# A different order of projection tiles in the second half of each group's round: B, C, x, x, z, z

## The chip, the core and the metric

The kernel runs on one core of one Trainium2 chip. The metric is the device time of one execution in microseconds (us); lower is better. TensorE (PE in the rows) does the matrix products, VectorE (DVE), ScalarE (ACT) and GpSimd (POOL) work on 128-partition tiles, and SyncE (SP) issues most transfers. Each engine works through its own list of instructions in order, and engines wait for each other by semaphores.

## What is computed

One layer of a diffusion trunk for 128 context and 1024 latent tokens, 1152 in all, of width 1024. What matters here is the mixer with its two branches, and how its inputs are made from one projection:

```python
proj = h @ lw["w_in"]
xbc, z, dt_raw, hq, hf, hi, hg, gate_logits = jnp.split(proj, cuts, axis=-1)
xbc = silu(depthwise_conv5(xbc) + conv_b)      # along a row of 64 tokens (latent)
xs, bm, cm = jnp.split(xbc, [...])             # x, B, C of the SSD branch
y = ssd_scan(xs, dt, a, bm, cm, s0)            # forward and backward, 8 groups
y = y * jax.nn.silu(z)
y = group_rmsnorm(y, ssd_norm_w)
o = hgrn2_scan(silu(hq), log_f, k, hi, s0)     # forward and backward, 8 heads
```

x, B and C go through a five-tap convolution and silu; z goes through silu alone. The convolution and the closing silu of x, B and C are elementwise work for ScalarE and VectorE, some five times that of z.

## The kernel before

**Stages.** `setup` makes the normalised input `h` in a high and a low float part. `mixers` is the stage of this change. After it `merge_and_ffn` and `last_norm` do the output projections, the feed-forward part and the last norm; the change does not touch them.

**Rounds and slots.** `mixers` goes over 8 groups, seven in a hardware loop (`Fori`) and the last one written out behind it. A round has a first half, stage A, and a second half, stage B, of 18 slots each. In every slot TensorE first computes one *unit* of projection (`project`: a 128-column weight tile times 384 tokens, as 24 matmuls, eight slices of the contraction times three combinations of high and low parts) and then a slice of recurrent work. Three units make one *tile* of the projection, one weight tile over all 1152 tokens.

**What runs beside what.** In stage A the recurrent work is the SSD scan of this group (`ssd`), and the projections make the inputs of this group's HGRN branch. In stage B the recurrent work is the HGRN scan (`hgrn`), and the projections make z, B, C and x of the next group. The last group's stage B has no next group and projects gate columns, with a tanh in the place of the convolution. The HGRN work is 33 steps (`STEPS`), two in a slot (`slot_of`), so that it falls into three blocks of five slots: block 0 in slots 1 to 5, block 1 in slots 6 to 10, block 2 in slots 11 to 15; slots 16 and 17 hold little. For each step GpSimd makes the argument (L1665 to L1686), ScalarE its Exp (L1110), VectorE a product (L1474), TensorE a small matmul (L818), and VectorE merges the result (L1462, L1465). `hs_b` and `hs_f` are the chunk states; their updates (L1443) follow matmul L848. TensorE may run only two of the merged results ahead (`lv_used`, L815).

**How a unit of stage B is evacuated.** Two PSUM banks take the units in turn (`bank_free`). For a z unit ScalarE takes a tanh from the bank (L955) and VectorE multiplies it with the bank (L1310), which frees it. For a convolution unit ScalarE copies the bank to `pad` (L939), which frees it, and makes the first tap (L946); VectorE adds four taps (L1303); ScalarE takes the tanh of the result one slot later (`conv_tanh`, L921), before the Exps of that slot; VectorE closes with a product (`conv_silu`, L1290), before its HGRN work of that slot.

**The order around it.** All orders are written out by hand: `CONV_TILES` says which of the six tiles are convolved, `B_COLS` and `PRO_COLS` which columns are loaded in turn, `b_dest` where a tile goes. Weights come by SyncE into two buffers (`raw`), are cast to the high part by ScalarE (L914) and split by VectorE (L1277, once per tile in its second slot); TensorE waits for the split at the tile's first unit. At the start of stage B ScalarE makes `rstd` and VectorE norms y into `x_t` (`ssd_norm`, L1376), after which SyncE stores `x_t` (`stores`). At the end of stage B ScalarE makes the rstd of the HGRN branch (L1115, L1118), VectorE norms o (L1484, L1486), ScalarE stores it (L1123); only then do the loop's back edge and stage A of the next round come on ScalarE. Ahead of the loop a *prologue* makes dt and the same six tiles for group 0, without recurrent work beside them.

Of the kernel before, what the change touches and what calls it, by code (L numbers as in the profile page):

```python
# [12 lines left out]
P = 128  # L13
# [5 lines left out]
NB = 3  # L19
# [85 lines left out]
            eng.wait_ge(self.sem, self.g * self.per + (self.before + self.n))  # L105


CONV_TILES = (2, 3, 4, 5)


def conv_index(k):

    return k - 2 * NB


def b_tile(k):
# [77 lines left out]
def setup(nc, scope, sb, sem, m):  # L194
# [40 lines left out]
    with nc.Block() as block:  # L235
        @block.sync
        def _(sp):
            sp.dma_start(cst[:, :], m["cst_in"]).then_inc(consts_in, 16)
            sp.dma_start(junk[:, 0:LEVELS * P], m["masks_in"].rearrange("p l i -> p (l i)")).then_inc(masks_in, 16)

            def row(part, col, src, n):
                sp.dma_start(rows[part:part + n, col, :], src).then_inc(rows_in, 16)

            row(0, 0, m["ssd_conv_w"][0, 0:4, :].rearrange("k (t p) -> (k t) p", p=P), 128)
            row(0, 1, m["ssd_conv_w"][0, 4, :].rearrange("(t p) -> t p", p=P), 32)
            row(32, 1, m["ssd_conv_b"][0].rearrange("(t p) -> t p", p=P), 32)
            row(64, 1, m["ada_b"][0].rearrange("(t p) -> t p", p=P), 48)
            row(112, 1, m["norm_mix_w"][0].rearrange("(t p) -> t p", p=P), 8)
            row(120, 1, m["norm_ffn_w"][0].rearrange("(t p) -> t p", p=P), 8)
            row(0, 2, m["ssd_norm_w"][0].rearrange("(t p) -> t p", p=P), 16)  # L250
            row(16, 2, m["hgrn_norm_w"][0].rearrange("(t p) -> t p", p=P), 8)
            row(24, 2, m["c_in"][0].rearrange("(t p) -> t p", p=P), 8)
            row(32, 2, m["c_ctx"].rearrange("(t p) -> t p", p=P), 8)

            sp.dma_start(d_all[:, :], m["ssd_d"][0].rearrange("(a h) -> a h", a=1).broadcast_to([P, 32])
                         ).then_inc(rows_in, 16)
            def load_ada(j):
                sp.dma_start(ada[j % 3][:, :, :], ada_w[:, j * ADA_T * P:(j + 1) * ADA_T * P]
                             .rearrange("(k p) c -> p k c", p=P)).then_inc(ada_in[j % 3], 16)

            for c in range(3):
                sp.dma_start(xt[c][:, :], x_rows(c)).then_inc(x_in[c], 16)
                load_ada(c)

            for i, (col, n) in enumerate(((COL_DT, HD), (COL_Z, P))):
                sp.dma_start(raw[i][:, :, 0:n], m["w_src"](m["w_in"][0], col, n)).then_inc(m["w_landed"][i], 16)
            for j in range(3, ADA_N):
                sp.wait_ge(ada_used, j - 2)
                load_ada(j)
                if j < NC:  # L270
                    sp.wait_ge(x_turned, j - 2)
                    sp.dma_start(xt[j % 3][:, :], x_rows(j)).then_inc(x_in[j % 3], 16)
# [177 lines left out]
def mixers(nc, scope, sb, sem, m):  # L450
# [133 lines left out]
        n = TILES_BEFORE + t  # L584
        return n % 2, g * (TILES_GROUP // 2) + n // 2, g * TILES_GROUP + n

    PRO_COLS = [(COL_DT, 64), (COL_Z, P), (COL_Z + P, P), (COL_B, P), (COL_C, P), (COL_X, P), (COL_X + P, P)]

    A_COLS = [(COL_FF, P), (COL_FB, P), (COL_Q, P), (COL_G, P), (COL_GATE, P), (COL_I, P)]
    B_COLS = [(COL_Z, GW), (COL_Z + P, GW), (COL_B, P), (COL_C, P), (COL_X, GW), (COL_X + P, GW)]  # L590


    with nc.Block() as block:
        @block.sync
        def _(sp):
            def load(g, t, col, width=P):
                i, _, n = tile(g, t)
                if not (g is None and t < 2):
                    sp.wait_ge(w_split.sem, n - 1)
                sp.dma_start(raw[i][:, :, 0:width], w_src(w_in, col, width)).then_inc(w_landed[i], 16)  # L600

            def stage_a(g):
                for t, (base, step) in enumerate(A_COLS):
                    load(g, t, g * step + base)

            def stores(g, last):

                sp.wait_ge(y_final, g + 1)
                dst = y_dram[2 * g:2 * g + 2] if isinstance(g, int) else y_dram[bass.ds(g * 2, 2)]
                sp.dma_start(dst.rearrange("t p n -> p t n"), x_t[:, :, :]).then_inc(y_stored, 16)  # L610

                hs = slice(HPG * g, HPG * (g + 1)) if isinstance(g, int) else bass.ds(g * HPG, HPG)
                for d in range(2):
                    sp.dma_start(m["new_ssm"][0, 0, d, hs].rearrange("(t e) p n -> (e p) t n", e=2),
                                 st_in[:, 2 * d:2 * d + 2, :]).then_inc(so_stored, 16)

            def store_h(g):
                sp.wait_ge(kc_used.sem, kc_used.at(g, 4))
                hh = slice(g, g + 1) if isinstance(g, int) else bass.ds(g, 1)
                for d in range(2):  # L620
                    sp.dma_start(m["new_hgrn"][0, 0, d, hh].rearrange("a k v -> k (a v)"),
                                 so_h[:, d, :]).then_inc(soh_stored, 16)

            sp.dma_start(cols[:, 0:1], m["ssd_dt_bias"][0].rearrange("d (h a) -> (d h) a", a=1)
                         ).then_inc(cols_in, 16)
            sp.dma_start(cols[:, 1:2], m["ssd_a_log"][0].rearrange("d (h a) -> (d h) a", a=1)
                         ).then_inc(cols_in, 16)
            sp.dma_start(acc[0][:, 0:2 * P], m["neg_in"].rearrange("p d i -> p (d i)")).then_inc(cols_in, 16)
            for t, (col, _) in enumerate(PRO_COLS):
                if t >= 2:  # L630
                    load(None, t, col)

            with sp.Fori(0, G - 1) as g:
                stage_a(g)
                for t, (base, step) in enumerate(B_COLS):
                    if t == 4:
                        stores(g, False)
                    load(g, 6 + t, g * step + (base + step))
                store_h(g)
            g = G - 1  # L640
            stage_a(g)
            for t in range(8):
                if t == 4:
                    stores(g, True)
                load(g, 6 + t, COL_GATE + D + t * P)
            store_h(g)

            last_tile = tile(G - 1, 13)[2]
            for i in range(2):
                sp.wait_ge(w_split.sem, last_tile + i)  # L650
                slot = (last_tile + 1 + i) % 2
                sp.dma_start(raw[slot][:, :, :], w_src(m["w_ssd_out"][0, 0:D, :], slot * P)
                             ).then_inc(m["m_w_in"][slot], 16)
            sp.wait_ge(y_stored, 16 * G)

            sp.wait_ge(so_stored, 32 * G)
            sp.wait_ge(soh_stored, 32 * (G + 1))
            sp.wait_ge(o_stored, 16 * (G + 1))
            for i in range(2):
                sp.wait_ge(gate_stored[i], 16 * (G * (1 + i) + 4 * NB))  # L660
# [241 lines left out]
        def _(act):  # L902
# [20 lines left out]
            def b_evac(g, k):  # L923
# [24 lines left out]
                                   ).then_inc(tap_done.sem, 1)  # L948
                else:

                    if k >= 2:
                        act.wait_ge(bank_free[ui], used)
                    elif g is not None:
                        act.wait_ge(v_turned, g * NB + (k + 2))
                    act.activation(th[ui][:, :], bank[:, 0:BW], ACT.Tanh, scale=0.5).then_inc(th_ok.sem, 1)  # L955

            def b_th_free(g, k):

                ci = conv_index(k)
                if ci >= 2:  # L960
                    wait(silu_done, g, ci - 1)

            def a_evac(g, k):
                t, b = divmod(k, NB)
# [224 lines left out]
            for k in range(SLOTS):  # L1189
# [3 lines left out]
                b_evac(None, k)  # L1193
                if k % NB == 0:
                    high(None, k // NB + 2) if k < SLOTS - NB else high(0, 0)
            b_th_free(None, SLOTS - 1)
            conv_tanh(None, SLOTS - 1)
            act.wait_ge(dt_turned, 1)
            flat = tok[:, :, :, :].rearrange("p a c r -> p (a c r)")
            for i in range(4):  # L1200
# [7 lines left out]
            def stage_b(g):  # L1208
                for k in range(SLOTS):
# [10 lines left out]
                        hgrn_rstd(g)  # L1220
                    if k % NB == 0:
                        high(g, 6 + k // NB + 1)
                b_th_free(g, SLOTS - 1)
                conv_tanh(g, SLOTS - 1)
                store_o(g)

            with act.Fori(0, G - 1) as g:
# [32 lines left out]
        def _(dve):  # L1260
# [18 lines left out]

            def b_dest(k):  # L1280
                t, b = b_tile(k)
                return (z_t[:, 0, blk(b)], z_t[:, 1, blk(b)], b_t[:, blk(b)], c_t[:, blk(b)],
                        x_t[:, 0, blk(b)], x_t[:, 1, blk(b)])[t]

            def conv_silu(g, k):
                ui = b_unit(g, k)[0]
                wait(th_ok, g, k + (0 if g is None else 2 * NB) + 1)
                if k == 12 and g is not None:
                    dve.wait_ge(y_stored, g * 16 + 16)
                dve.scalar_tensor_tensor(b_dest(k), th[ui][:, :], 1.0, acc[ui][:, :], ALU.add,  # L1290
                                         ALU.mult).then_inc(silu_done.sem, 1)
# [254 lines left out]
            for k in range(SLOTS):  # L1546
# [2 lines left out]
                b_evac(None, k)  # L1549
                if k % NB == 1:  # L1550
                    low(None, k // NB + 2) if k < SLOTS - NB else low(0, 0)
            conv_silu(None, SLOTS - 1)
            ch = dve_s

            with dve.Fori(0, G - 1) as g:
                ch.round(g)
                stage_a(g)
                for k in range(SLOTS):
# [7 lines left out]
                        hgrn_norm(g)  # L1566
                    if k % NB == 1:
                        low(g, 6 + k // NB + 1)
                conv_silu(g, SLOTS - 1)
                assert ch.n == DVE_ROUND, ch.n  # L1570
            g = G - 1
            ch.round(g)
# [627 lines left out]
```

## Time and profile before

| | us |
|---|---|
| median of 3 runs | 3678.38 (3676.9 to 3679.32) |
| span of the profiled execution | 3671.7 |
| TensorE busy | 3388.0 (92%) |
| VectorE busy | 1775.6 (48%) |
| ScalarE busy | 1386.3 (38%) |
| GpSimd busy | 810.5 (22%) |
| mean granted clock of TensorE | 0.971 |

The profiled execution took its span of 3671.7 us; the median is 6.7 us above that, which lies around the span. The busy shares are means over stages with different limits: the mixer stage lies between about 145 and 2352 us of the span, and seven of its eight rounds have convolutions in stage B. In a timeline row the first two numbers are the start and the time that the instruction or a merged run of them took; what stands in brackets is the idle time of the engine before it and what ended it. In a row of stretches the numbers are the length, then the busy time of each engine.

### The profile page before, as it was taken

To read this page: it belongs to the slowest core of one execution; us is meant where nothing else is said; L and a number is where in the kernel's file an instruction comes from. 1 tells how busy PE (TensorE), PEld (TensorE's weight loads), DVE (VectorE), ACT (ScalarE), POOL (GpSimd) and SP (SyncE) were. 2 spreads that over 40 slices of the span, in tenths; PEclk is the share of its full clock that TensorE was granted. 3 is DMA by queue.
4 is the path that set the end of the run, shared out by engine and by line. 5 is a ranking of instruction groups with operands and counts; after the bars stand their busy time and mean duration, and the time that the engine had idled before them with its cause. 6 is when DMAs were issued, how large, how long until landed. Compare 5 with 4: busy or idle time off the path is not lost. (4 is left out here: it accounts for less than half of the span.)

```text
span 3671.7 us, 56487 instructions
## 1 busy us (share of the span) xinstructions
PE 3388.0 (92%) x19856; PEld 3225.1 (88%) x19856; DVE 1775.6 (48%) x2918; ACT 1386.3 (38%) x2655; POOL 810.5 (22%) x1138
## 2 busy tenths in 40 slices
PE   7789989989989889899899899899998999999997
PEld 2379979889889889889889899799997999999997
DVE  2455566556656746745755764334434222222233
ACT  4334444454554454454544545321124110120112
POOL 0002532532622613524425325000010000000000
PEclk9999999999999999999999999999998999999998
DMA  8310111111111111111111112344231111111111
GB/s 312 102 35 24 47 41 28 45 40 30 43 34 30 45 37 44 32 31 53 29 31 47 40 30 70 121 143 135 84 87 50 40 40 46 40 40 40 46 35 73
DMA packets 284854, 213.08 MB, mean 58 GB/s; under 512 B 10152, under 2 KB 266576, under 8 KB 284624
## 3 DMA queue, kind: packets, MB, share of 16 engines
q1 hardware_dynamic: 239808, 159.80, 14.5%
q10 hardware_dynamic: 44816, 50.35, 4.4%
q8 instruction: 128, 2.10, 0.2%
q14 instruction: 102, 0.84, 0.1%
HBM read 173.94 MB, written 36.18 MB: 57 GB/s over the span
## 5 line engine op out<-in xcount | busy, mean ns | idle before, releaser
L676 PE MATMUL bank<-h_hi,w_hi 128*128 128x384 f32 (+1 forms) x2520 | 892.5, 354 | 38.5 <-DVE z_t L1310 19.1
L676 PE MATMUL bank<-h_lo,w_hi 128*128 128x384 f32 (+1 forms) x2520 | 857.6, 340 | 0.0
L676 PE MATMUL bank<-h_hi,w_lo 128*128 128x384 f32 (+1 forms) x2520 | 856.6, 340 | 0.0
L676 PEld LDWEIGHTS bank<-h_hi,w_hi 128*128 128x128 f32 (+1 forms) x2520 | 484.6, 192 | 48.5 <-DVE z_t L1310 19.4
L1858 PE MATMUL bank<-a_hi,v_hi 128*128 128x384 f32 x1440 | 490.6, 341 | 33.8 <-DVE v_lo L1959 12.2
L676 PEld LDWEIGHTS bank<-h_lo,w_hi 128*128 128x128 f32 (+1 forms) x2520 | 483.3, 192 | 5.8
L1858 PE MATMUL bank<-a_lo,v_hi 128*128 128x384 f32 x1440 | 485.8, 337 | 0.0
L1858 PE MATMUL bank<-a_hi,v_lo 128*128 128x384 f32 x1440 | 485.7, 337 | 0.0
L676 PEld LDWEIGHTS bank<-h_hi,w_lo 128*128 128x128 f32 (+1 forms) x2520 | 481.9, 191 | 1.3
L1858 PEld LDWEIGHTS bank<-a_hi,v_hi 128*128 128x128 f32 x1440 | 273.3, 190 | 46.9 <-issue 35.6
L1858 PE MATMUL bank<-b_hi,v_hi 128*128 128x384 f32 x912 | 304.7, 334 | 0.5 <-DVE v_lo L1959 0.5
L1858 PE MATMUL bank<-b_hi,v_lo 128*128 128x384 f32 x912 | 304.6, 334 | 0.0
L1858 PE MATMUL bank<-b_lo,v_hi 128*128 128x384 f32 x912 | 304.6, 334 | 0.0
L1303 DVE SCALAR_TENSOR_TENSOR acc<-pad,taps,acc 128x384 f32<-128x384 f32 x384 | 274.2, 714 | 61.6 <-ACT acc L946 51.1
L1858 PEld LDWEIGHTS bank<-a_lo,v_hi 128*128 128x128 f32 x1440 | 274.2, 190 | 0.0
L1858 PEld LDWEIGHTS bank<-a_hi,v_lo 128*128 128x128 f32 x1440 | 273.9, 190 | 0.0
L1110 ACT ACTIVATE qk<-qk 128x768 f32<-128x768 f32 (+1 forms) x240 | 180.6, 777 | 187.8 <-POOL qk L1685 176.1
L1881 ACT ACTIVATE v_hi<-raw 128x1024 fp32r<-128x1024 f32 x99 | 104.8, 1059 | 295.4 <-PE bank L1858 289.2
L818 PE MATMUL bank<-qk 128*128 128x128 f32 x1008 | 142.0, 286 | 69.4 <-DVE at L1462 24.4
L818 PEld LDWEIGHTS bank<-qk 128*128 128x128 f32 x1008 | 132.7, 197 | 77.5 <-DVE at L1462 27.9
L1623 POOL TENSOR_TENSOR xp<-xb,tok_g 128x256 f32<-128x256 f32 x128 | 81.7, 646 | 500.2 <-PE bank L757 305.7
L2014 DVE TENSOR_TENSOR small<-small,bank 128x384 f32<-128x384 f32 x66 | 36.6, 554 | 295.4 <-PE bank L1858 295.4
(270 smaller groups left out, 5499.3 us busy)
## 6 DMA issues: line engine op xcount, KB each, us to landing
raw<-in_w_in SPq DMA_DIRECT2D x104, 512.0 KB, 3.9
raw<-in_ffn_w SPq DMA_DIRECT2D x60, 512.0 KB, 3.8
ada<-in_ada_w SPq DMA_DIRECT2D x12, 2048.0 KB, 9.3
small<-gate_scratch ACTq DMA_DIRECT2D x72, 192.0 KB, 2.4
gate_scratch<-th ACTq DMA_DIRECT2D x48, 192.0 KB, 1.9
y_scratch<-x_t SPq DMA_DIRECT2D x8, 1152.0 KB, 6.9
small<-y_scratch ACTq DMA_DIRECT2D x48, 192.0 KB, 2.4
raw<-in_w_ssd_out SPq DMA_DIRECT2D x16, 512.0 KB, 4.1
```

Source lines behind the costliest of these rows:

```text
L676: last = pe.matmul(out, w[i][:, k, 0:cols_n], h[:, k, blk(hb)], start=(k == 0 and j == 0), stop=(k == KT - 1 and j == 2))
L818: last = pe.matmul(S[(i + 1) % 3][:, chunk(j)], q[:, 1, chunk(j)], rhs, start=True, stop=True)
L1110: last = act.activation(v, v, ACT.Exp)
L1303: ins = dve.scalar_tensor_tensor(out, pad[b][:, :, j:j + GRID], taps[:, ti, j:j + 1], out, ALU.mult, ALU.add)
L1623: return pool.tensor_tensor(out.rearrange("p (h c) -> p h c", c=HD), x.rearrange("p (h c) -> p h c", c=HD), w.rearrange("p (h a) -> p h a" ...
L1858: last = pe.matmul(banks[3 * s + b][:, 0:BW], wp[s][:, k, :], operand[ap][:, k, blk(b)], start=(k == 0 and j == 0), stop=(k == kt - 1 and ...
L1881: act.activation(w_hi[s][:, :, :], raw[s][:, :, :], ACT.Copy).then_inc(w_high, 1)
L2014: dve.tensor_tensor(tmp[b][:, :], gate[b][:, :], bank, ALU.mult).then_inc(freed, 1)
```

## The change

In stage B and in the prologue the six tiles come as B, C, x, x, z, z, where they came as z, z, B, C, x, x. The four convolved tiles are then units 0 to 11 of the stage and z is units 12 to 17. What follows from it in the code:

- the column lists `PRO_COLS` and `B_COLS`, the first `COL_Z` load in `setup`, and `b_dest` are reordered;
- the store of y stands before the third load of a stage B on SyncE instead of before the fifth, since x is now written from unit 6 on;
- a convolution unit at the start of stage B (k of 0 and 1) waits in `b_th_free` for the turned v that z waited for; the first two z units wait in `b_evac` for the last two `conv_silu` instead;
- the last `conv_tanh` and `conv_silu`, which stood after the last slot, are gone: their unit now closes in slot 12.

No operation is added or left out, and the number of waits is about the same.

```diff
-CONV_TILES = (2, 3, 4, 5)
+CONV_TILES = (0, 1, 2, 3)
 def conv_index(k):
-    return k - 2 * NB
+    return k
...
-    PRO_COLS = [(COL_DT, 64), (COL_Z, P), (COL_Z + P, P), (COL_B, P), (COL_C, P), (COL_X, P), (COL_X + P, P)]
+    PRO_COLS = [(COL_DT, 64), (COL_B, P), (COL_C, P), (COL_X, P), (COL_X + P, P), (COL_Z, P), (COL_Z + P, P)]
-    B_COLS = [(COL_Z, GW), (COL_Z + P, GW), (COL_B, P), (COL_C, P), (COL_X, GW), (COL_X + P, GW)]
+    B_COLS = [(COL_B, P), (COL_C, P), (COL_X, GW), (COL_X + P, GW), (COL_Z, GW), (COL_Z + P, GW)]
...
-                    if t == 4:
+                    if t == 2:
                         stores(g, False)
...
-                    if k >= 2:
+                    if k >= 4 * NB + 2:
                         act.wait_ge(bank_free[ui], used)
-                    elif g is not None:
-                        act.wait_ge(v_turned, g * NB + (k + 2))
+                    else:
+                        wait(silu_done, g, k - 1)
...
                 if ci >= 2:
                     wait(silu_done, g, ci - 1)
+                elif g is not None:
+                    act.wait_ge(v_turned, g * NB + (k + 2))
...
-                b_th_free(g, SLOTS - 1)
-                conv_tanh(g, SLOTS - 1)
                 store_o(g)
```

On VectorE, the start of stage B in the loop, from the norm of y (`x_t`) to the split of the next weights (`w_lo`). Before, slots 0 and 1 hold one product `z_t` each between the HGRN products `qk`:

```order
L1376 SCALAR_TENSOR_TENSOR x_t<-x_t,vec_g,me 128x1152 x2
...
L1474 TENSOR_TENSOR qk1<-qk1,q_t 128x384
L1264 REGISTER_ALU
L1310 SCALAR_TENSOR_TENSOR z_t<-th1,bank1 128x384
L1264 REGISTER_ALU
L1474 TENSOR_TENSOR qk2<-qk2,q_t 128x384
...
L1310 SCALAR_TENSOR_TENSOR z_t<-th0,bank0 128x384
L1276 REGISTER_ALU
L1277 TENSOR_TENSOR w_lo0<-raw0,w_hi0 128x1024
```

And of the change, the same stretch (four taps `acc` in each slot, of which the last of each slot stands here, and the closing product of B):

```order
L1374 SCALAR_TENSOR_TENSOR x_t<-x_t,vec_g,me 128x1152 x2
...
L1301 SCALAR_TENSOR_TENSOR acc1<-pad2,taps,acc1 128x384
L1262 REGISTER_ALU
L1288 SCALAR_TENSOR_TENSOR b_t<-th1,acc1 128x384
L1262 REGISTER_ALU
L1472 TENSOR_TENSOR qk2<-qk2,q_t 128x384
...
L1301 SCALAR_TENSOR_TENSOR acc0<-pad1,taps,acc0 128x384
L1274 REGISTER_ALU
L1275 TENSOR_TENSOR w_lo0<-raw0,w_hi0 128x1024
L1262 REGISTER_ALU
L1288 SCALAR_TENSOR_TENSOR b_t<-th0,acc0 128x384
L1262 ISA
```

Eight taps and two closing products have taken the place of two products `z_t`, ahead of the first updates of `hs_b`. (The line numbers of the changed kernel are two or more lower here for VectorE and two higher for ScalarE.)

On ScalarE, the start of stage B in the loop; `ktok` are the turned keys that TensorE waits for. Before:

```order
L955 ACTIVATE th1<-bank1 128x384
L911 ISA
L913 ISA
L914 ACTIVATE w_hi0<-raw0 128x1024
L906 REGISTER_ALU
L1077 ACTIVATE ktok0<-bank4 128x384
```

And of the change:

```order
L939 ACTIVATE pad2<-bank1 128x6x64
L941 REGISTER_ALU
L942 REGISTER_ALU
L946 ACTIVATE acc1<-pad2,taps 128x384
L911 ISA
L913 ISA
L914 ACTIVATE w_hi0<-raw0 128x1024
L906 REGISTER_ALU
L1079 ACTIVATE ktok0<-bank4 128x384
```

A first tap has come ahead of the keys, and the tanh of that unit (L921, not shown) now follows the four keys and stands before the next Exps.

On ScalarE, the end of stage B in the loop, before, where the last tanh of a convolution stands between the rstd of the HGRN branch and the store of o:

```order
L946 ACTIVATE acc0<-pad0,taps 128x384
L906 REGISTER_ALU
L1115 ACT_TABLE_LOAD
L1115 ACTIVATE g_t<-g_t,cst 128x1152
L105 REGISTER_ALU
L1118 ACT_TABLE_LOAD
L1118 ACTIVATE g_t<-g_t 128x1152
L906 REGISTER_ALU
L921 ACTIVATE th0<-acc0 128x384
```

In the changed kernel the tanh of the last z unit stands straight before that rstd, and there is none behind it:

```order
L955 ACTIVATE th0<-bank0 128x384
L906 REGISTER_ALU
L1117 ACT_TABLE_LOAD
L1117 ACTIVATE g_t<-g_t,cst 128x1152
L105 REGISTER_ALU
L1120 ACT_TABLE_LOAD
L1120 ACTIVATE g_t<-g_t 128x1152
```

## Rows read from the trace of the kernel before

**Rows 1.** The page: head and busy times.

```profile
span 3671.7 us, 56487 instructions
PE 3388.0 (92%) x19856; PEld 3225.1 (88%) x19856; DVE 1775.6 (48%) x2918; ACT 1386.3 (38%) x2655; POOL 810.5 (22%) x1138
```

**Rows 2.** Groups by line: busy us, mean ns | idle before, releasers.

```profile
L676 PE MATMUL bank<-h_hi,w_hi 128*128 128x384 f32 (+1 forms) x2520 | 892.5, 354 | 38.5 <-DVE z_t L1310 19.1 <-DVE w_lo L1277 14.6 <-ACT dec L1205 4.8
...
L1303 DVE SCALAR_TENSOR_TENSOR acc<-pad,taps,acc 128x384 f32<-128x384 f32 x384 | 274.2, 714 | 61.6 <-ACT acc L946 51.1
...
L1310 DVE SCALAR_TENSOR_TENSOR z_t<-th,bank 128x384 f32<-128x384 f32 x48 | 26.3, 549 | 40.6 <-ACT th L955 40.6
```

**Rows 3.** Stretches, stage B of the second group: stretch length, PE, PEld, DVE, ACT, POOL, PEclk.

```profile
668.30:702.70 34.40, 31.32 (x212) 30.81 (x211) 22.32 (x39) 15.62 (x27) 25.81 (x36) 1.00 0.25 78
...
716.10:739.90 23.80, 19.67 (x120) 19.16 (x119) 21.04 (x31) 10.59 (x20) 10.96 (x14) 0.93 0.11 29
...
746.50:755.30 8.80, 6.01 (x39) 5.69 (x37) 6.37 (x11) 5.66 (x12) 8.56 (x13) 1.00 0.16 45
755.30:776.40 21.10, 19.36 (x116) 18.84 (x116) 19.02 (x31) 9.12 (x17) 2.71 (x2) 0.92 0.10 26
776.40:786.50 10.10, 9.24 (x54) 8.66 (x52) 5.21 (x8) 4.19 (x11) 0.00 (x0) 1.00 0.01 2
```

**Rows 4.** Stretches, the same slots of the last group's stage B, without convolutions.

```profile
2271.40:2288.90 17.50, 17.50 (x119) 17.50 (x119) 9.14 (x13) 7.05 (x11) 9.96 (x15) 1.00 0.25 76
...
2295.50:2301.30 5.80, 5.80 (x39) 5.66 (x37) 3.11 (x7) 2.80 (x5) 4.06 (x8) 1.00 0.10 34
2301.30:2318.50 17.20, 17.20 (x117) 17.20 (x116) 6.32 (x10) 5.71 (x9) 4.24 (x6) 1.00 0.27 82
2318.50:2327.50 9.00, 9.00 (x53) 8.73 (x52) 1.22 (x1) 5.25 (x8) 0.00 (x0) 1.00 0.28 88
```

**Rows 5.** Timeline of ACT, slot 0 of that stage B, keys and Exps of slot 1.

```profile
673.62 0.47 ACT L955 ACTIVATE th<-bank 128x384 f32<-128x384 f32 x1
...
674.93 1.62 ACT L1077 ACTIVATE ktok<-bank 128x384 f32<-128x384 f32 x4
...
676.63 1.60 ACT L1110 ACTIVATE qk<-qk 128x768 f32<-128x768 f32 x2
```

**Rows 6.** Timeline of DVE, slots 0 to 2: norm of y, states, first merge.

```profile
667.55 3.17 DVE L1376 SCALAR_TENSOR_TENSOR x_t<-x_t,vec_g,me 128x1152 f32<-128x1152 f32 x2 [16.25 <-ACT me L1066]
...
680.57 1.58 DVE L1443 SCALAR_TENSOR_TENSOR hs_b<-hs_b,hdec,bank 128x128 f32<-128x128 f32 x4
...
683.00 0.55 DVE L1462 TENSOR_TENSOR at<-bank,cst 128x384 f32<-128x384 f32 x1
```

**Rows 7.** Timeline of PE, the waits that end slots 1 and 2.

```profile
675.47 1.60 PE L818 MATMUL bank<-qk 128*128 128x128 f32 x12 [2.72 <-ACT ktok L1077]
...
683.61 0.60 PE L818 MATMUL bank<-qk 128*128 128x128 f32 x3 [0.36 <-DVE at L1462]
```

**Rows 8.** Timeline of DVE: four taps with POOL idle, four with POOL busy.

```profile
514.21 2.58 DVE L1303 SCALAR_TENSOR_TENSOR acc<-pad,taps,acc 128x384 f32<-128x384 f32 x4
...
717.66 3.96 DVE L1303 SCALAR_TENSOR_TENSOR acc<-pad,taps,acc 128x384 f32<-128x384 f32 x4
```

**Rows 9.** Timeline of ACT, the end of stage B into stage A, first round.

```profile
525.60 0.50 ACT L939 ACTIVATE pad<-bank 128x384 f32<-128x384 f32 x1
526.14 0.71 ACT L946 ACTIVATE acc<-pad,taps 128x384 f32<-128x384 f32 x1
...
539.20 0.38 ACT L1017 ACTIVATE s_f<-bank 128x256 f32<-128x256 f32 x1 [6.88 <-issue]
```

**Rows 10.** Timeline of PE, the wait in slot 1 of stage A, second round.

```profile
540.67 0.45 PE L683 MATMUL bank<-cst,x_t 128*128 128x128 f32 x2 [4.85 <-ACT xb L1025]
```

**Rows 11.** Stretch just behind that wait: length, PE busy, ..., PEclk.

```profile
541.60:548.50 6.90, 6.90 (x37) 6.79 (x35) 1.23 (x1) 4.45 (x10) 0.28 (x1) 0.80 0.30 77
```

**Rows 12.** The page: DMA issues, KB each, us to landing.

```profile
y_scratch<-x_t SPq DMA_DIRECT2D x8, 1152.0 KB, 6.9
```

More of the change, by code:

```diff
@@ L263, in _ @@
                 load_ada(c)
-            for i, (col, n) in enumerate(((COL_DT, HD), (COL_Z, P))):
+            for i, (col, n) in enumerate(((COL_DT, HD), (COL_B, P))):
                 sp.dma_start(raw[i][:, :, 0:n], m["w_src"](m["w_in"][0], col, n)).then_inc(m["w_landed"][i], 16)
@@ L1195, in _ @@
                     high(None, k // NB + 2) if k < SLOTS - NB else high(0, 0)
-            b_th_free(None, SLOTS - 1)
-            conv_tanh(None, SLOTS - 1)
             act.wait_ge(dt_turned, 1)
@@ L1281, in b_dest @@
                 t, b = b_tile(k)
-                return (z_t[:, 0, blk(b)], z_t[:, 1, blk(b)], b_t[:, blk(b)], c_t[:, blk(b)],
-                        x_t[:, 0, blk(b)], x_t[:, 1, blk(b)])[t]
+                return (b_t[:, blk(b)], c_t[:, blk(b)], x_t[:, 0, blk(b)], x_t[:, 1, blk(b)],
+                        z_t[:, 0, blk(b)], z_t[:, 1, blk(b)])[t]
             def conv_silu(g, k):
@@ L1287, in conv_silu @@
                 wait(th_ok, g, k + (0 if g is None else 2 * NB) + 1)
-                if k == 12 and g is not None:
+                if k == 2 * NB and g is not None:
                     dve.wait_ge(y_stored, g * 16 + 16)
@@ L1551, in _ @@
                     low(None, k // NB + 2) if k < SLOTS - NB else low(0, 0)
-            conv_silu(None, SLOTS - 1)
             ch = dve_s
@@ L1568, in _ @@
                         low(g, 6 + k // NB + 1)
-                conv_silu(g, SLOTS - 1)
                 assert ch.n == DVE_ROUND, ch.n
```

## The prediction

> **What bounds the kernel now.** I read the page first, then the groups of instructions by line, the waits of TensorE, and then the stages as stretches, slot by slot. TensorE is busy 3388.0 of 3671.7 us [rows 1], so a change of order can only act through the moments at which TensorE waits, or runs at a lower granted clock. For one of them the last round serves as a control, since its stage B runs the same HGRN slots without convolutions. Slots 8 to 10 take 23.8 us in the second group's stage B and 17.5 us in the last group's [rows 3, 4]: 6.3 us more, of which 1.7 us is a granted clock of 0.93 (0.07 of 23.8). Slot 12 takes 8.8 against 5.8 us (+3.0), slots 13 to 15 take 21.1 against 17.2 (+3.9), slots 16 and 17 take 10.1 against 9.0 (+1.1) [rows 3, 4]. In the control TensorE is busy without a gap in all of these. So a convolution beside an HGRN block costs TensorE time. VectorE shows why: it is busy 21.04 of the 23.8 us, against 9.14 of 17.5 [rows 3, 4]; it owes TensorE the HGRN products and merges, and pays them late. Six of these expensive slots with convolutions have z instead after the change, and six cheap ones get convolutions.
>
> **Part 1: block 0 gets the convolutions (slots 0 to 5).** Without them it takes 34.4 us, with VectorE busy 22.32 of it and GpSimd 25.81 [rows 3]. Two ways lead to its new length.
>
> By load: a convolution unit gives VectorE four taps of 714 ns, 2.86 us [rows 2]; its closing product has the shape of z's (549 ns) and replaces it. Five units are 14.3 us, and 22.32 + 14.3 = 36.6 us no longer fits 34.4: at least +2.2 us even with VectorE never idle. At the share of 0.88 at which it works in slots 8 to 10 (21.04 of 23.8), 36.6 us take 41.6, +7.2 us. Taps are also not 714 ns there: four take 2.58 us with GpSimd idle and 3.96 us beside it [rows 8], and in block 0 GpSimd works 75% of the time. With 3.96 us each the load is 22.3 + 19.8 = 42.1 us, at 0.88 47.8 us, +13.4 us.
>
> By chain: the start is more exposed than the other blocks. In slot 0 ScalarE now makes pad and first tap (0.5 and 0.71 us, [rows 9]) where one tanh of 0.47 us stood, so the keys at 674.93 [rows 5] come 0.7 us later; TensorE already waits 2.72 us for them [rows 7]: +0.7 us. In slot 1 ScalarE must wait for VectorE's first taps, which end at about 677.7 (first tap ready at 674.8, then 2.6 to 3.3 us), then makes the tanh (0.5), two Exps (1.60, [rows 5]), and the second unit's pad and tap (1.2), so that VectorE can start its second four taps at about 681.0. With 3.3 us for them (between 2.58 and 3.96), 1.2 for the split of the weights and 0.55 for the closing product, the chain of `hs_b` that started at 680.57 [rows 6] starts at about 686.1, 5.5 us later, and the first merge behind it, at 683.00, with it. TensorE waits only 0.36 us for that merge now [rows 7] and would wait some 5 us: the end of slot 2 moves by 5.4 us, the 0.7 included. Slots 3 to 5 hold the same step kinds as slots 8 to 10, so I take their +6.3. Together +11.7 us. This lies between the load's 7.2 and 13.4 and nearer to the latter, since GpSimd is busier here than in any other block. I take **+11.7**, bounds +4 (the load bound of 2.2, and some chain) and +16. What is queued behind the new waits: on ScalarE the load of the HGRN states and the Exps, for which VectorE's products and so TensorE wait; on VectorE the split of the next tile's weights, which moves from 680.6 to about 685.5 and is needed at the end of slot 2, so it is hidden by the longer slot 2.
>
> **Part 2: block 1 keeps them.** Its units are convolutions before and after: 0. VectorE enters it with a lag, but slots 5 and 6 hold few merges and absorb it. Slot 12 still sees the last convolution (unit 11), so its +3.0 stays.
>
> **Part 3: the end of stage B gets z.** Slots 13 to 17 lose 3.9 and 1.1 us [rows 3, 4]: **-5.0**. The control has no z product there; one of 549 ns a unit [rows 2] stays in for z, on a VectorE that has room (6.32 busy of 17.2, [rows 4]). Bounds -3.5 (part of it is clock, 0.92 of 21.1 us is 1.7) and -6.
>
> **Part 4: the turn into stage A.** ScalarE's last unit needs pad and tap before the rstd tables (1.2 us, [rows 9]) and then only a tanh of 0.47 to 0.49: 0.9 us earlier with everything behind it, the norm of o, its store, and the back edge; the copy at 539.20 had waited 6.88 us, named as issue [rows 9]. TensorE waits 4.85 us for the product of that chain [rows 10] and takes the gain in full: **-0.9**. The tanh and the closing product after the last slot were not in this chain. That stage A needs x_t, B and C at its first slots is no term: TensorE shows no wait there for `conv_silu`.
>
> **Part 5: SyncE's queue.** The load of the third tile, the first of x, now stands behind the store of y, which waits for `y_final`, at 667.55 + 3.17 = 670.7 [rows 6]. The store lands in 6.9 us [rows 12]; with as much again for the load, which is less than half as large, the weights are there at 684.5. The cast that needs them comes in slot 3, which began after the merge at 683.61 [rows 7] and will begin some 5 us later. Cost 0, covered by those 5 us; beyond them each us would be one of TensorE's.
>
> **Part 6: the prologue, once.** TensorE waits 19.1 us there for the first z product [rows 2]. That wait ends some 3 us earlier, as ScalarE's copy frees the bank instead; the first convolutions then start behind the dt chain and hold up the weight splits by about as much. At its end TensorE waits 4.8 us for `dec` [rows 2], behind the last tanh; with z last about 2 of them go. Net **-1**, bounds -5 and +5.
>
> **Part 7: the clock.** Behind the 4.85 us gap the granted clock is 0.80 over 6.9 us: 1.4 us lost [rows 10, 11]. The new gap in slot 2 is about as long, so I add 1.4 us x 7; the gap of part 4 shrinks to 3.95 us, for which I take back half of its loss: **+0.7** a round, bounds -2 and +3.
>
> **Sum.** A looped round: 11.7 - 5.0 - 0.9 + 0.7 = +6.5 us; seven of them +45.5, and -1 for the prologue: +44. The last round's stage B does not change. The profiled execution would take 3671.7 + 44 = 3716; with the 6.7 us that lie around the span, 3678.4 + 44 = **3722 us**, slower by 1.2%.
>
> **A rule weighed.** Four taps take 1.4 us longer beside GpSimd than alone [rows 8]. The Trainium skill, SBUF, "Who interferes with whom", says that a VectorE instruction with two SBUF inputs and a GpSimd instruction that reads SBUF exclude each other, and one with a single SBUF input does not. A tap reads pad and acc, both in SBUF; z's product reads one operand from PSUM. By that rule GpSimd's 25.8 us in block 0 and five times four taps at 2.58 us, 12.9 us, would have to be laid end to end: 38.7 us, +4.3 at least, on both engines. The rows agree in direction; the sum above does not use it.
>
> **Rivals.**
> *Hidden in idle VectorE (faster).* VectorE is idle for 12.1 of block 0's 34.4 us [rows 3], and GpSimd with 25.8 busy may be the pace-setter, so that convolutions fill holes. If block 0 grows by 2.8 us only (the load bound of 2.2 and little more), a round gains 3.1 us and the kernel takes 3656. It decides below +5.9 us for block 0, where parts 3 and 4 balance it. Against it: the holes are waits for ScalarE and GpSimd, the taps would stand ahead of what TensorE needs next, and in slots 8 to 10 the same mixture did not hide. Chance 0.12.
> *A draw.* Block 0 grows by 5 to 6.8 us, near the load figure of 7.2: the round changes by -0.9 to +0.9, 3671 to 3684. Chance 0.13.
> *A heavier start.* The port shared with GpSimd slows the arguments too, block 0 grows by 16, and the lag runs on into block 1: 7 x 4.3 more, 3752. Chance 0.15, of which 0.05 beyond 3756.
> *The late weights.* If the store holds up the x tile past its cover, say by 3 us in each round: +21, 3743. Chance 0.05.
>
> The forecast has 0.55. Its own range is 3690 to 3750: block 0 between +8 and +15. **Range**: 3672 (the draw included) to 3756; it leaves out the faster rival and the far end of the heavy start. Within 0.2% (7.4 us, about what can be told from no change): 0.13. Faster: 0.12. Slower: 0.75.
>
> **What the profile of the changed kernel would show.** The seven looped stages B grow by some 6 us each; slots 1 to 5 from 34.4 to some 46, slots 13 to 15 shrink from 21.1 to about 17. TensorE waits several us at L818 for the first merge in slot 2, where it waited 0.36. VectorE's taps in block 0 are nearer to 1 us than to 0.62. The wait at L683 in stage A shrinks by 0.9. The prediction is wrong if slots 1 to 5 grow by less than 6 us, if slots 13 to 17 do not shrink, or if a wait for weights appears on TensorE at the x tiles.

## The result, and the profile after

The change makes the kernel slower by 1.9%: 3747.15 us as the median of four runs (3738.78 to 3749.67) against 3677.68 us (3676.9 to 3679.32) of the kernel before beside them, ratio 1.0185, 95% interval 1.0171 to 1.0200. The forecast was 3722 us, with a range of 3672 to 3756: the direction holds and the time lies in the range, but the loss is 69.5 us and not 44. The profiled execution went from 3671.7 us [rows 1] to 3744.6, +72.9.

The page of after: its head, the busy times, and the group of VectorE's taps (busy us, mean ns | idle time before them and what ended it).

```profile
span 3744.6 us, 56495 instructions
PE 3422.3 (91%) x19856; PEld 3260.0 (87%) x19856; DVE 1802.6 (48%) x2918; ACT 1387.9 (37%) x2655; POOL 837.5 (22%) x1138
...
L1301 DVE SCALAR_TENSOR_TENSOR acc<-pad,taps,acc 128x384 f32<-128x384 f32 x384 | 292.9, 763 | 38.0 <-ACT acc L946 27.5
```

TensorE is busy 34 us longer than in [rows 1], though it does the same matmuls, and its mean granted clock is 0.961 and not 0.971: part of the longer time is spent in matmuls at the lower clock. The taps take 763 ns each, not 714 [rows 2].

**Where it went.** The seven looped stages B as stretches: length, then busy time of PE, PEld, DVE, ACT, POOL. The sum of the kernel before:

```profile
sum 876.70, PE 772.20 PEld 748.58 DVE 612.29 ACT 434.04 POOL 476.31; mean PE 110.31 PEld 106.94 DVE 87.47 ACT 62.01 POOL 68.04
```

and of after, with the second group's stage ahead of it:

```profile
671.00:807.10 136.10, 115.62 (x691) 112.35 (x689) 93.59 (x140) 63.06 (x112) 71.46 (x92) 0.94 0.15 41
...
sum 950.30, PE 801.62 PEld 778.81 DVE 657.14 ACT 442.49 POOL 504.30; mean PE 114.52 PEld 111.26 DVE 93.88 ACT 63.21 POOL 72.04
```

The whole loss is in these stages: +73.6 us, 10.5 a round. TensorE's busy time grows by 29.4 of them and its time not busy by the other 44.2. The eight stages A together are 3.4 us shorter, the loop begins 1.6 us later (0.5 of it ahead of the prologue's first matmul), and 1.1 us more lie at the end.

TensorE's waits over the whole span (us in total, times, longest), before:

```profile
PE bank L683 <- ACT xb L1025: 30.4, 7, 4.9
PE bank L818 <- DVE at L1465: 27.8, 20, 2.6
PE bank L818 <- DVE at L1462: 24.4, 18, 2.8
PE bank L818 <- ACT ktok L1077: 22.5, 8, 3.4
PE bank L829 <- DVE at L1465: 21.6, 14, 2.2
```

and after. L1460 is here the merge that stood at L1462, L1463 the masked copy that stood at L1465:

```profile
PE bank L818 <- DVE at L1460: 58.8, 21, 6.8
PE bank L829 <- DVE at L1463: 33.0, 14, 3.3
PE bank L818 <- ACT ktok L1079: 28.2, 8, 3.5
PE bank L683 <- ACT xb L1027: 25.5, 7, 4.3
PE bank L818 <- DVE at L1463: 21.2, 15, 2.7
```

The four HGRN waits grow from 96.3 to 141.2 us, +44.9, which is the time not busy. The largest is the wait for the merge, from 24.4 to 58.8.

Stretches of after in the second group's stage B (columns as in [rows 3], which they answer): slot 1, slot 2, slots 3 and 4, slot 5, then slots 13 to 15 and 16 to 17.

```profile
678.00:690.30 12.30, 8.75 (x51) 8.43 (x49) 7.47 (x10) 6.88 (x14) 12.30 (x17) 0.86 0.52 171
690.30:703.50 13.20, 8.64 (x51) 8.45 (x50) 12.31 (x21) 4.97 (x10) 9.01 (x11) 0.87 0.15 42
703.50:715.40 11.90, 11.32 (x75) 11.13 (x74) 10.23 (x20) 6.45 (x12) 3.10 (x5) 1.00 0.00 0
715.40:725.80 10.40, 7.39 (x45) 7.07 (x43) 10.05 (x15) 3.74 (x8) 4.86 (x7) 0.90 0.19 52
779.20:797.60 18.40, 18.40 (x117) 18.40 (x116) 9.06 (x15) 4.58 (x8) 1.97 (x2) 0.93 0.12 30
797.60:807.10 9.50, 9.17 (x52) 8.58 (x50) 1.69 (x2) 2.08 (x5) 0.00 (x0) 1.00 0.16 39
```

Slots 1 to 5 take 47.8 us where they took 34.4 [rows 3]. Over all seven rounds, the mean of each slot by the start of its first projection matmul:

| slots | before | after | difference |
|---|---|---|---|
| 1 | 10.43 | 11.96 | +1.5 |
| 2 | 7.31 | 13.82 | +6.5 |
| 3 and 4 | 11.03 | 11.85 | +0.8 |
| 5 | 6.06 | 10.25 | +4.2 |
| 6 to 12 | | | within 0.6 each |
| 13 to 17 | 30.9 | 28.0 | -2.9 |

Slot 2 is where the forecast said. Its chain on VectorE, timeline of after (start, length):

```profile
690.27 1.57 DVE L1472 TENSOR_TENSOR qk<-qk,q_t 128x384 f32<-128x384 f32 x2 [1.18 <-ACT qk L1112]
692.14 3.08 DVE L1301 SCALAR_TENSOR_TENSOR acc<-pad,taps,acc 128x384 f32<-128x384 f32 x4 [0.29 <-ACT acc L946]
695.13 1.22 DVE L1275 TENSOR_TENSOR w_lo<-raw,w_hi 128x1024 fp32r<-128x1024 f32 x1
696.27 0.86 DVE L1288 SCALAR_TENSOR_TENSOR b_t<-th,acc 128x384 f32<-128x384 f32 x1
697.05 2.35 DVE L1441 SCALAR_TENSOR_TENSOR hs_b<-hs_b,hdec,bank 128x128 f32<-128x128 f32 x6
699.32 0.55 DVE L1460 TENSOR_TENSOR at<-bank,cst 128x384 f32<-128x384 f32 x1
```

and on TensorE, the end of slot 1 and the end of slot 2 (projections left out):

```profile
685.95 2.79 PE L818 MATMUL bank<-qk 128*128 128x128 f32 x12 [3.55 <-ACT ktok L1079]
...
699.92 1.65 PE L818 MATMUL bank<-qk 128*128 128x128 f32 x6 [4.56 <-DVE at L1460]
701.36 2.38 PE L848 MATMUL bank<-v_tok,ktok 128*128 128x128 f32 x12
```

Four taps, the split of the weights and the convolution's closing product stand ahead of the six updates of `hs_b` and the merge, and TensorE waits 4.56 us for that merge (0.36 in [rows 7]). VectorE has no gap from 692.14 to the merge, so this is its own work in its own order. Stage B starts 9.7 us later here than before (671.0 against 661.3), so in the time of before the updates start at 687.4; the forecast had 686.1. Most of that 1.3 us arises on ScalarE, between the tanh, which ends at 688.34, and the Exps at 689.42. There it issues the loads of the HGRN states and makes two short copies:

```profile
689.18 0.22 ACT L1099 ACTIVATE hdec<-f_t 128x9 f32<-128x9 f32 x1 [0.85 <-issue]
```

The lower clock shows in the same rows. Behind the wait of 3.55 us the twelve products at L818 take 2.79 us; in the kernel before they took 1.60, behind a wait of 2.72 [rows 7].

**What the lower clock costs, and where it costs nothing.** In the third round slot 1 runs at full clock (first row) and slot 2 does not (second row). The wait for the merge is then longer than the 4.56 us above:

```profile
949.49:960.17 10.68, 7.13 (x51) 6.81 (x50) 7.04 (x9) 5.77 (x10) 10.68 (x15) 1.00 0.55 184
960.17:975.90 15.73, 8.95 (x52) 8.76 (x50) 13.64 (x22) 6.08 (x13) 11.75 (x14) 0.79 0.16 44
```

```profile
972.04 1.65 PE L818 MATMUL bank<-qk 128*128 128x128 f32 x6 [6.78 <-DVE at L1460]
```

Slot 1 takes from 10.7 to 13.1 us in the seven rounds, but VectorE starts the merge 21.0 to 21.9 us after the start of slot 1 in all of them (14.6 to 14.7 in the kernel before). So what slot 1 loses by the lower clock is taken off the wait in slot 2, and the two slots together are no shorter when slot 1 is fast: 26.4 us in the third round, 25.5 in the second. What is not covered is the work behind the merge: from the end of that wait to the end of slot 2 the second round takes 3.58 us (699.92 to 703.50), at the lower clock, where the kernel before took 2.03. The 8.2 us of slots 1 and 2 in that round are thus 6.65 us of a later merge and 1.55 us of lower clock behind it.

### The profile page after: what moved, and what is told of

Same layout as the page of the kernel before. It is cut to its first block and busy times, and to the rows that moved or that the text cites. A ratio compares the mean times of both kernels' runs of the same rounds, so it can differ in the third digit from the quotient of the medians.

```text
span 3744.6 us, 56495 instructions
## 1 busy us (share of the span) xinstructions
PE 3422.3 (91%) x19856; PEld 3260.0 (87%) x19856; DVE 1802.6 (48%) x2918; ACT 1387.9 (37%) x2655; POOL 837.5 (22%) x1138
## 5 line engine op out<-in xcount | busy, mean ns | idle before, releaser
L1301 DVE SCALAR_TENSOR_TENSOR acc<-pad,taps,acc 128x384 f32<-128x384 f32 x384 | 292.9, 763 | 38.0 <-ACT acc L946 27.5
L818 PE MATMUL bank<-qk 128*128 128x128 f32 x1008 | 149.6, 296 | 104.4 <-DVE at L1460 58.8
L818 PEld LDWEIGHTS bank<-qk 128*128 128x128 f32 x1008 | 139.2, 206 | 112.3 <-DVE at L1460 62.8
L1678 POOL TENSOR_TENSOR qk<-f_t 128x192 f32<-128x192 f32 x168 | 124.8, 743 | 301.0 <-PE bank L808 149.1
```

The source lines that it names most:

```text
L818: last = pe.matmul(S[(i + 1) % 3][:, chunk(j)], q[:, 1, chunk(j)], rhs, start=True, stop=True)
L1301: ins = dve.scalar_tensor_tensor(out, pad[b][:, :, j:j + GRID], taps[:, ti, j:j + 1], out, ALU.mult, ALU.add)
L1678: pool.tensor_tensor(q_up, f_up, rf, ALU.subtract)
```

## Experiments

The theory: VectorE works through its list in order, and the taps that now stand in block 0 delay the HGRN work that TensorE waits for. The rivals: the changed ScalarE work (pad and first tap ahead of the keys), the place of the store of y, or simply a load that any six slots with convolutions would show.

**Without the taps.** Three of the four taps that VectorE does per convolution are left out, in both orders, so these two kernels compute another convolution.

```diff
-ACT_ROUND, DVE_ROUND, DT_ACT, DT_DVE = 11, 112, 7, 19
+ACT_ROUND, DVE_ROUND, DT_ACT, DT_DVE = 11, 76, 7, 19
...
-                    for j in range(1, TAPS):
-                        if j > 1:
+                    for j in (TAPS - 1,):
+                        if j < 0:
```

> The kernel before, with three of VectorE's four taps of each convolution left out (the work is changed, so the time is that of less work). Theory V (VectorE's taps, in its one queue with the HGRN products and merges, are what a convolution costs TensorE): the seven looped stages B lose most of their 14.9 us over the control of the last round, some 10 to 12 us each, so about 3600 us. Theory S (the cost is ScalarE's: first tap, copy and the tanh that waits): they lose under 5 us each, 3645 or more.

> The changed kernel with the same three taps left out. Theory V: the 70 us between the two orders shrink to under 20 us, so 3600 to 3620; in slot 2 TensorE's wait for the first merge falls from 4.6 us to about 1 us. Theory S: the difference stays above 45 us, since the first tap ahead of the keys and the tanh ahead of the Exps are still there.

Measured: the old order 3569.6 us (ratio to before 0.9712, 0.9696 to 0.9729), the new one 3584.39 (0.9757, 0.9740 to 0.9773). Both gained more than expected. The distance between the orders falls from 70 to 14.8 us: the three taps carry 55 us of it. In the new order the wait for the merge is small and the wait for the keys is what it was (TensorE's waits of that kernel):

```profile
PE bank L818 <- ACT ktok L1079: 28.2, 8, 3.5
...
PE bank L818 <- DVE at L1460: 7.7, 6, 2.7
...
PE bank L829 <- DVE at L1463: 1.1, 7, 0.2
```

This pair also shows what the later keys do to slot 1. Slot 1 of the second group as a stretch, first in the old order, then in the new:

```profile
648.11:657.97 9.86, 7.13 (x51) 6.81 (x50) 4.85 (x6) 6.15 (x13) 9.86 (x15) 1.00 0.05 14
```

```profile
645.74:658.04 12.30, 8.76 (x52) 8.44 (x50) 6.21 (x9) 8.41 (x16) 11.87 (x17) 0.86 0.52 171
```

The products behind the wait in that slot, again old and new:

```profile
655.27 1.60 PE L818 MATMUL bank<-qk 128*128 128x128 f32 x12 [2.73 <-ACT ktok L1077]
```

```profile
653.71 2.85 PE L818 MATMUL bank<-qk 128*128 128x128 f32 x12 [3.54 <-ACT ktok L1079]
```

The keys come 0.81 us later, and the slot is 2.44 us longer: 1.63 us of it are the same matmuls at a granted clock of 0.86 instead of 1.00. But this is not what is left of the loss. Slots 1 and 2 together are 3.2 us longer a round (20.5 against 17.3 in the mean; with all taps 8.0, 25.8 against 17.7), and that is again the merge: VectorE starts it 17.6 to 17.9 us after the start of slot 1, where the old order has 14.5. VectorE's merge in the old order, then VectorE's merge and TensorE's wait for it in the new one:

```profile
662.63 0.55 DVE L1462 TENSOR_TENSOR at<-bank,cst 128x384 f32<-128x384 f32 x1
```

```profile
663.63 0.55 DVE L1460 TENSOR_TENSOR at<-bank,cst 128x384 f32<-128x384 f32 x1
```

```profile
664.23 0.94 PE L818 MATMUL bank<-qk 128*128 128x128 f32 x6 [1.11 <-DVE at L1460]
```

Slot 1 starts at 648.11 in the one and 645.74 in the other. Where slot 1 keeps its full clock, in the seventh round of the new order, the wait for the merge is 2.69 us and the two slots take 21.1 us, not less. How much of the 3.2 us is the remaining tap and the closing product, and how much ScalarE's pad and first tap ahead of them, no run here takes apart.

**The store of y at its old place** (new order otherwise).

```diff
-                    if t == 2:
+                    if t == 4:
                         stores(g, False)
```

> The changed kernel with the store of y and of the states before the fifth load of a stage B on SyncE, as in the kernel before, instead of before the third. Theory V: the store's place costs nothing, 3747 within 4 us. Rival (SyncE's queue holds up the weights of the first x tile): 10 us or more faster.

Measured: 3744.74 us, ratio 1.0192 (1.0175 to 1.0209), within the spread of the changed kernel's own times. The place of the store costs nothing that can be told from noise, as forecast.

**Convolutions in slots 0 to 2 alone, or out of them alone.** Two further orders of the tiles, each moved in all tables: B, z, z, C, x, x, and z, B, C, x, x, z.

```diff
-    B_COLS = [(COL_Z, GW), (COL_Z + P, GW), (COL_B, P), (COL_C, P), (COL_X, GW), (COL_X + P, GW)]
+    B_COLS = [(COL_B, P), (COL_Z, GW), (COL_Z + P, GW), (COL_C, P), (COL_X, GW), (COL_X + P, GW)]
```

> Order B, z, z, C, x, x: one convolved tile in slots 0 to 2, z in slots 3 to 8, the other convolutions in slots 9 to 17 as before. Start theory: slots 1 and 2 alone take the 8 us a round that they take in the change (26 against 18 us); slots 7 and 8 give back 1 and 3 us, slot 5 stays at 6.1 us: 4 us a round, about 3705. Load rival (each convolution beside HGRN costs the same): within 7 us of the kernel before, as nine of the twelve do not move.

```diff
-    B_COLS = [(COL_Z, GW), (COL_Z + P, GW), (COL_B, P), (COL_C, P), (COL_X, GW), (COL_X + P, GW)]
+    B_COLS = [(COL_Z, GW), (COL_B, P), (COL_C, P), (COL_X, GW), (COL_X + P, GW), (COL_Z + P, GW)]
```

> Order z, B, C, x, x, z: slots 0 to 2 hold z as before, slots 15 to 17 hold z as in the change, convolutions in slots 3 to 14. Start theory (what costs most is the chain of slots 1 and 2, where the merges stand behind the taps of the second unit and the clock falls in the gap): slots 1 and 2 take 18 us as before and not 26, and a round lies 2 to 5 us above that of the kernel before: 3692 to 3715. Load rival (a convolution beside HGRN costs the same in any slot, and only how many there are counts): 12 slots with HGRN as in the change, 3735 to 3750.

Measured: B first 3694.72 us (1.0045, 1.0028 to 1.0062), less than my theory gave and more than the load rival; z at both ends 3704.35 (1.0075, 1.0058 to 1.0092). With B first, slots 1 and 2 take 25.2 us, nearly as in after (25.8), and slots 3 to 9 are cheap as z slots are; the largest wait of the kernel is that for the merge (there L1467):

```profile
PE bank L818 <- DVE at L1467: 49.5, 14, 6.7
```

With z first, slots 1 and 2 stay as in the kernel before and slot 5 takes 10.5 us in the mean where it took 6.06; the wait for the masked copy (there L1466) before the products at L829 leads:

```profile
PE bank L829 <- DVE at L1466: 44.6, 21, 3.3
```

So block 0's loss in after (+13.0 a round) is made of two separate places: +7.5 in slots 1 and 2 in the one kernel, +4.4 in slot 5 in the other. A load that is alike in any six slots would not do that: slots 3 and 4 cost 0.8 us in after with a convolution beside each.

**Another order on the two engines.** If VectorE's order is the cause, putting the HGRN work ahead of the convolution's last step should win much of the loss back. In stage B ScalarE's Exps for the next slot go ahead of the tanh, and VectorE's HGRN work goes ahead of the closing product; the taps stay where they are.

```diff
+                    hgrn_exp(g, k + 1)
                     if k > 0 and (k - 1) // NB in CONV_TILES:
                         b_th_free(g, k - 1)
                         conv_tanh(g, k - 1)
-                    hgrn_exp(g, k + 1)
...
+                    hgrn(g, k + 1)
                     if k > 0 and (k - 1) // NB in CONV_TILES:
                         conv_silu(g, k - 1)
-                    hgrn(g, k + 1)
```

> The changed kernel with one thing more: in each slot of stage B ScalarE makes the Exps before the tanh of the last convolution, and VectorE does its HGRN work before that convolution's closing product. Nothing is added or taken away. Chain theory (what TensorE waits for is the merge behind taps, tanh and closing product in order, so taking tanh and closing product out of its way helps): the merge of slot 2 comes 2 us earlier and those of the other slots about 1 us: 3695 to 3715. Load theory (VectorE has too much to do in block 0, whatever the order in a slot): 3740 or more.

> The kernel before with the same exchange in each slot of stage B. Chain theory: the waits in slots 8, 10, 12, 13 and 15 shrink by about 1 us each, so 4 to 6 us a round, 3635 to 3650, and the two orders then differ by less than 65 us. Load theory: within 7 us of the kernel before.

> Order z, B, C, x, x, z with that exchange. Chain theory: 4 to 6 us a round faster than without it (3704), so 3662 to 3676. Load theory: 3700.

Measured: on the new order 3705.28 us (1.0074, 1.0057 to 1.0091), 42 less; on the old order **3652.82 us** (0.9931, 0.9914 to 0.9947), 25 less than before and the fastest that does the whole computation, though expected a little lower still; on z at both ends 3677.83 (0.9993, 0.9984 to 1.0003), just above the expected range. The waits, new order with the swap, then old order with the swap:

```profile
PE bank L818 <- DVE at L1460: 37.0, 19, 5.0
...
PE bank L829 <- DVE at L1463: 24.9, 12, 3.2
```

```profile
PE bank L818 <- DVE at L1465: 35.1, 21, 3.0
...
PE bank L818 <- DVE at L1462: 12.0, 11, 1.6
PE bank L829 <- DVE at L1465: 9.3, 14, 1.6
```

The same swap takes 21.8 us from the wait for the merge in the new order and 12.4 in the old one. The orders still differ by 52 us: the taps themselves remain ahead of the updates, and the keys are as late. Nor is the gain on the new order one of slots 1 and 2 alone: of 5.7 us a round, 1.9 lie there and 3.8 in slots 6 to 17, where the old order gains too.

**The halves of the swap**, each alone on the new order.

> The changed kernel with ScalarE's half of the exchange alone: Exps before the tanh of the last convolution; VectorE's order as in the change. The full exchange gave 42 us. If what TensorE waits for is mostly the products behind late Exps, this half gives most of it: 3705 to 3720. If it is the merges behind the closing product, the tanh now comes even later and this half gives nothing or loses: 3740 to 3765. I expect the second, 3750.

> The changed kernel with VectorE's half alone: HGRN updates, merges and products before the closing product of the last convolution; ScalarE's order as in the change. If the merges behind the closing product are what counts, 3705 to 3720, and the two halves add up to the full exchange; if the Exps count, 3735 or more. I expect the first, 3715.

Measured: ScalarE's half alone 3787.75 us (1.0307, 1.0284 to 1.0329), VectorE's half alone 3716.12 (1.0101, 1.0084 to 1.0119). Against the changed kernel that is +41 and -31, and both together -42: the halves do not add up. (The changed kernel was not timed again beside these runs; the kernel before moved by up to 4.3 us between the groups of runs.) TensorE's waits, ScalarE's half and then VectorE's:

```profile
PE bank L818 <- DVE at L1460: 75.7, 21, 6.7
PE bank L829 <- DVE at L1463: 50.1, 14, 4.8
```

```profile
PE bank L818 <- DVE at L1460: 42.1, 21, 4.7
PE bank L829 <- DVE at L1463: 32.8, 14, 3.5
```

With ScalarE's half alone the tanh comes later, and VectorE stands at the closing product (L1288), in order, waiting for it, with the merges behind: a loss larger than I had expected. It lies in slots 5, 7 and 10 (+1.0, +3.1 and +3.4 us a round), while slots 1 and 2 are 0.7 shorter. VectorE's idle time at L1288, in us and times, in the changed kernel and then with ScalarE's half:

```profile
  ACT th L921: 42.5, 64
```

```profile
  ACT th L921: 145.2, 78
```

Once VectorE's HGRN work stands ahead of that point, the same edit on ScalarE helps by 11 us. This is the strongest evidence for the mechanism: TensorE's time follows what stands ahead of the merge in VectorE's list, and what VectorE waits for there, and not how much VectorE does. Its instructions are the same in these kernels, and with VectorE's half it is busy longer than in the changed kernel (1812.8 against 1802.6 us) while the kernel is faster.

## Why the prediction was right, and where it was off

**The direction and the mechanism (part 1): right.** Block 0 pays more than the end of stage B gives back. The replay of slot 2's chain held within 1.3 us on VectorE; it had left out the state loads and copies on ScalarE (1.1 us). The wait was 4.56 us where "some 5" stood, and the keys' wait rose by 0.83 us (forecast 0.7). With the clock term of part 7 the forecast has 13.1 us for slots 1 to 5, and they grew by 13.0 in the mean. That this fits so well is partly luck, since two errors cancel: slots 1 and 2 took 8.0 us, not 5.4 + 1.4, and slots 3 to 5 took 5.0, not 6.3, 4.2 of it in slot 5. I had taken the 6.3 over as a whole from slots 8 to 10, where TensorE waits twice in the second round, 2.6 us in slot 8 and 1.5 in slot 10; in slots 3 to 5 of the changed kernel the first of these is 0.6 us, and the other, for the masked copy, 3.0. The taps were expected nearer to 1 us than to 0.62 in block 0; in slots 0 to 5 they take 0.775 in the mean.

**The end of stage B (part 3): right sign, too large, and the largest miss.** Slots 13 to 17 gave 2.9 us and not 5.0, which over seven rounds is 14.7 of the 28 us that the profiled span lies above its forecast (72.9 against 44.5). Slot 13 gave 0.5: the low clock that follows slot 12's gap is still there (0.93 over slots 13 to 15, with TensorE busy throughout), since unit 11 is a convolution in both orders. I had named this as a bound and not taken it. In slots 16 and 17 I took the loop's end for a convolution's cost: they gave 0.1 us and not 1.1. Slot 17 takes 5.0 to 5.5 us in the first six looped rounds of after, with no convolution beside it, and 4.46 in the seventh, which has no back edge behind it. The control, the last round, has none either, so it was no control for the last slot. Behind the second round's back edge, for one, TensorE waits 0.38 us for nothing that the profile shows.

**The clock (part 7): right in slot 2, wrong in stage A.** The 1.4 us that I charged for the gap in slot 2 are close to the 1.55 measured behind it. TensorE's busy time in the stages B grew by far more, 29.4 us or 4.2 a round, 17.1 of them in slots 1 and 2 (121.0 against 103.9 us). But busy time is not cost: slot 1's part of it comes ahead of the wait for the merge and shortens it. How much of the rest costs time, the split into busy and not busy does not tell. The time not busy grew by 44.2 us, where parts 1 and 3 give 7 x 6.7 = 46.9 (each holds 1.7 us of clock, with opposite signs). What failed is the half that I gave back in stage A: TensorE's busy time in the eight stages A did not fall but rose by 1.4 us (1024.7 to 1026.1).

**Block 1 (part 2): right.** Slots 6 to 12 moved by at most 0.6 us each, slot 6 by the lag of slot 5; slot 12 takes 8.78 us as before.

**Stage A (part 4): right for the wait, not for the stage.** The wait at L683 fell from 30.4 to 25.5 us, 0.7 a round where 0.9 was forecast. With the clock that part 7 gave back the stages A were to be 11.2 us shorter, and they are 3.4 us shorter: 7.8 us of the miss. The six that stand between looped stages B gain some 1 us each; the eighth takes 137.0 us where it took 134.3, with TensorE busy 3.0 us longer.

**SyncE (part 5): right**, shown by the run with the store at its old place.

**The prologue (part 6): wrong sign, small.** +1.6 us and not -1. The waits did move as said; the largest now is

```profile
PE bank L676 <- ACT pad L939: 16.2, 1, 16.2
```

where 19.1 stood [rows 2]. But the two units behind it took 10.3 and 6.8 us where they took 6.1 and 4.2, some 7 us more. Between them stands the hold-up of a weight split that part 6 had named, about as long as the gain; VectorE reaches the split behind the first taps (timeline of TensorE, prologue):

```profile
199.27 0.69 PE L676 MATMUL bank<-h_hi,w_hi 128*128 128x384 f32 x1 [3.31 <-DVE w_lo L1275]
```

The matmul behind it takes 0.69 us and the next fifteen 0.52 each, where the fast ones take 0.34: the rest of the 7 us is the lower clock, which I had not counted here.

**The rivals.** That idle VectorE hides the taps is out: in the changed kernel VectorE is idle for 7.7 of slots 1 to 5's 47.8 us in the second group, and TensorE waits all the same. The heavier start is what the time came nearest to, but the lag did not run on into block 1 as that rival had it, and slots 1 to 5 did not grow by 16. Of the rule that a VectorE instruction with two SBUF inputs and a GpSimd instruction that reads SBUF exclude each other (the Trainium skill, SBUF — State Buffer, "Who interferes with whom"): the taps slowed from 714 to 763 ns, and GpSimd is busy 28 us longer in the stages B with the same instructions, so the rows agree in direction. Without three of the taps GpSimd is busy 13.7 us less in the stages B of the new order (490.6 against 504.3). No run here takes GpSimd's work away from beside the taps, so how much of the 13.0 us this makes stays open.

## What to carry to other kernels

When work that nobody waits for soon moves in an engine's in-order list, ask first what stands behind it there and who waits for that: here the same VectorE work costs 70 us more in one order than in the other, and a swap of two calls on each of two engines gains 25 us in the cheaper one. Price a new wait on TensorE with the clock behind it, but only up to the next wait for another engine: what the clock takes ahead of such a wait shortens it, and costs nothing as long as the wait is the longer. So a rise of TensorE's busy time over identical work is a sign to look, and not yet a price. A round without the work in question is a good control only for slots that are the same in everything else, the loop's edge included.

## What the runs showed of the hardware

In the pair without the three taps a wait longer by 0.8 us (2.73 to 3.54) goes with a slot longer by 2.4 us in the second round, as the matmuls behind the wait ran at the lower of the two clock levels: twelve products took 2.85 us instead of 1.60. It is no fixed charge, and the wait alone does not decide it. In the kernel before the keys' wait is 2.72 us in all seven looped rounds, and slot 1 keeps a clock of 1.00 in four of them (9.9 us) but has 0.85 to 0.89 in the first, third and sixth (11.0 to 11.5 us). In the changed kernel it is 3.54 us in all seven, and slot 1 has 0.78 or 0.86 in five of them, but keeps 1.00 in the third and the seventh (10.7 us instead of 12.3). There slot 2 falls to 0.79 and takes 15.7 us instead of 13.2, most of it in a longer wait for the merge (6.78 us instead of 4.56); the two slots together come out 0.8 to 0.9 us longer than in the other rounds. So of the 73.6 us that this reordering cost in the stages B 29.4 stand in TensorE's busy time, in no list of waits, and a part of these was covered by waits that it would have had anyway.
